# Pairs of feed-forward weight strips multiplied with seven block products in place of eight

## The chip, the core and the metric

The kernel runs on one core of one Trainium2 chip. The engines run on their own and wait for each other by semaphores: TensorE (PE; PEld is its weight load), VectorE (DVE), ScalarE (ACT), GpSimd (POOL), and SyncE (SP), which issues most transfers. Times are device microseconds from one execution of the program; of several, the median counts.

## The reference

One inference step of a trunk of two layers on 640 tokens (128 context, 512 latent), width 1024. A layer is a modulated norm, three token mixers side by side, a gated sum with an output projection, and then the part that the change touches:

```python
    h2 = modulated_norm(x, norm_ffn, shift2, scale2)
    f_gate, f_up = jnp.split(h2 @ w_ffn_in, 2, axis=-1)
    x = x + gate2[:, None, :] * ((jax.nn.silu(f_gate) * f_up) @ w_ffn_out)
```

`w_ffn_in` is 1024 x 5632 and `w_ffn_out` 2816 x 1024, all in float32. shift, scale and gate are six parts of `mod`, a product of the conditioning with `w_ada`.

## The kernel before

Tokens lie along the free axis (T = 640, two halves of 320) and features on the partitions, in KD = 8 blocks of 128. Weights come as 292 strips of 128x1024, each eight 128x128 blocks, through three buffers `wraw`, issued by SyncE in order (`strip_load`, L437); a strip waits until the one three before it is in use. For accuracy each float32 operand is split in a high part (rounded to fp32r) and a low part (the rest), and a product is three matmuls: high x high, high x low, low x high. GpSimd makes both parts of a strip: the copy L481 and the subtraction L483, whose result lies on `wraw` itself. For eight strips of layer 0's mixers ScalarE makes the high part (`HI_ON_ACT`).

The feed-forward stage of a layer works on 22 products c, in two parts f of 11. Product c takes a gate strip and an up strip, each 8 blocks x 3 matmuls x 2 halves = 48 matmuls into a pair of PSUM banks (`tiles_of`, L499). ScalarE takes the SiLU (L1401), VectorE multiplies by the up part (`gact`, L1915), ScalarE makes its high part `ahi` (L1403) and VectorE the low part `alo` (L1918). After 11 products come 11 strips of `w_ffn_out`, and VectorE adds each block m of the result to x (`add_to_x`, L1872). The first two strips of the stage run block by block behind the norm (`first_strips`, L509); the last block of the stage is done one half after the other (`last_tile`, also L509), so that the next norm can begin: its squares are summed on VectorE (L1432), and TensorE spreads the root (`norm_spread`, L578). In the norm VectorE scales (`tn`, L1451), ScalarE writes `hhi` (L1019) and VectorE `hlo` (L1461).

The modulation is computed by VectorE reductions over 128x1024 rows of `w_ada` (`ada_dot`, L1483), two for each of 48 blocks per layer. They stand in layer 0's mixers and, 48 blocks of them, in the feed-forward stages (`LATE`: the last 8 of layer 0 and 40 of layer 1 in layer 0's stage, the last 8 of layer 1 in layer 1's). Their loads are issued from ScalarE's queue.

All orders are written out by hand in each engine's program.

## Time and profile before

| | us |
|---|---|
| median of 3 timed runs (lowest, highest) | 2983.67 (2977.31, 2991.55) |
| profiled execution | 2975.47 |
| its span, first to last instruction | 2973.6 |
| PE busy in the span | 2823.4 (95%) |
| POOL, DVE, ACT busy | 1596.7, 1430.7, 754.1 |
| mean granted TensorE clock | 0.974 |

The page lists busy time by engine, then the chain of work that ended last, then groups of instructions by line. A duration on it is one profiled execution's. An engine's busy time counts waiting that happens inside an instruction, as for a port; the chain counts what the end waited for. In names such as `L483 POOL TENSOR_TENSOR wlo<-wraw,whi` the result stands ahead of the arrow. A strip product's stage is best read from a stretch that holds only it: 1146 to 1589 us is the feed-forward of layer 0, 967 to 1100 the merge and the output projection ahead of it.

### The profile page before, as it was taken

How to read it: one execution, taken by the hardware profiler on the slowest of the kernel's cores; microseconds unless marked ns; L12 is line 12 of the kernel's file. 1: busy time of each engine (PE TensorE's matmuls, PEld its weight loads, DVE VectorE, ACT ScalarE, POOL GpSimd, SP SyncE). 2: the span in 40 equal slices, each digit the busy share in tenths (PEclk: the TensorE clock that was granted, in tenths of full speed). 3: DMA queues.
4: the chain of work that ended last, by engine and by line, in shares of the span. 5: the costliest groups of instructions: out<-in, count | busy, mean ns of one | idle time of the engine just before them, and what ended most of it. 6: DMA issues, size and time to landing. Idle time of an engine off the chain costs nothing.

```text
span 2973.6 us, 42669 instructions
## 1 busy us (share of the span) xinstructions
PE 2823.4 (95%) x17704; PEld 2550.6 (86%) x17704; DVE 1430.7 (48%) x2267; ACT 754.1 (25%) x1411; POOL 1596.7 (54%) x596
## 2 busy tenths in 40 slices
PE   7889899989999999999999989999999999999998
PEld 2349687978888999999998869797988998999998
DVE  6555685664545235477646571542455425411113
ACT  3442112215564112000112110414555212000110
POOL 0426132364434776788875507075333675777775
PEclk9979999999999999999999999899999999999999
DMA  5422242231111323345422213021111233322222
GB/s 218 138 96 95 92 161 88 96 92 43 52 46 61 114 70 123 113 156 163 144 91 88 92 59 102 5 93 54 46 52 52 84 96 107 98 73 78 72 78 79
DMA packets 80093, 272.12 MB, mean 92 GB/s; under 512 B 8955, under 2 KB 14715, under 8 KB 78108
## 3 DMA queue, kind: packets, MB, share of 16 engines
q1 hardware_dynamic: 48124, 168.77, 17.8%
q10 hardware_dynamic: 31776, 100.62, 9.8%
q8 instruction: 140, 2.29, 0.3%
q14 instruction: 53, 0.43, 0.1%
HBM read 245.76 MB, written 23.59 MB: 91 GB/s over the span
## 4 chain that ended last, share of the span: by engine, by line
PE 80%; DVE 9%; ACT 4%; issue 2%; DVEq 1%; DMA 1%; POOLq 1%; POOL 1%; ACTq 0%; SPq 0%
PE PS L499 46%; PE PS L843 9%; PE PS L562 4%; PE PS L636 3%; PE PS L892 2%; PE PS L509 2%; PE PS L790 2%; DVE adap L1483 2%; PE PS L864 1%; PE PS L774 1%; POOLq L482 1%; PE PS L602 1%; POOL wlo L483 1%; PE PS L759 1%; PE PS L869 1%
## 5 line engine op out<-in xcount | busy, mean ns | idle before, releaser
L481 POOL TENSOR_SCALAR whi<-wraw 128x1024 fp32r<-128x1024 f32 x284 | 819.2, 2884 | 1146.6 <-PE PS L499 635.5
L483 POOL TENSOR_TENSOR wlo<-wraw,whi 128x1024 fp32r<-128x1024 f32 x292 | 734.4, 2515 | 83.3 <-ACT whi L1246 38.9
L499 PE MATMUL PS<-hhi,whi 128*128 128x320 f32 x2432 | 556.7, 310 | 15.7 <-POOL wlo L483 15.7
L499 PE MATMUL PS<-hhi,wlo 128*128 128x320 f32 x2432 | 554.7, 309 | 0.0
L499 PE MATMUL PS<-hlo,whi 128*128 128x320 f32 x2432 | 554.7, 309 | 0.0
L499 PEld LDWEIGHTS PS<-hhi,whi 128*128 128x128 f32 x2432 | 407.2, 188 | 18.4 <-POOL wlo L483 11.5
L499 PEld LDWEIGHTS PS<-hlo,whi 128*128 128x128 f32 x2432 | 407.8, 188 | 0.0
L499 PEld LDWEIGHTS PS<-hhi,wlo 128*128 128x128 f32 x2432 | 407.4, 188 | 0.0
L1483 DVE CUSTOM_DVE_ANT_0 adap<-ada,cond 128x1024 f32<-128x1024 f32 x176 | 333.2, 1893 | 36.1 <-DMA ada<-in_w_ada 14.7
L1401 ACT ACTIVATE silu<-PS 128x640 f32<-128x640 f32 x44 | 31.2, 708 | 659.1 <-PE PS L499 655.8
L1915 DVE TENSOR_TENSOR gact<-silu,PS 128x640 f32<-128x640 f32 x44 | 36.1, 821 | 333.3 <-ACT silu L1401 333.3
L1872 DVE SCALAR_TENSOR_TENSOR x<-PS,mod,x 128x128 f32<-128x128 f32 x144 | 54.9, 435 | 249.2 <-PE PS L499 241.2
L1315 ACT ACTIVATE dp<-PS,mx 128x640 f32<-128x640 f32 (+1 forms) x160 | 113.5, 710 | 238.5 <-DVE mx L1772 238.4
L1772 DVE TENSOR_REDUCE mx<-PS 128x2 f32<-128x1280 f32 (+1 forms) x80 | 102.2, 1278 | 145.8 <-PE PS L870 93.4
L843 PE MATMUL PS<-hhi,whi 128*128 128x320 f32 x512 | 172.2, 336 | 0.0
L843 PE MATMUL PS<-hhi,wlo 128*128 128x320 f32 x512 | 158.6, 310 | 0.0
L843 PE MATMUL PS<-hlo,whi 128*128 128x320 f32 x512 | 158.5, 310 | 0.0
L499 PE MATMUL PS<-ahi,whi 128*128 128x320 f32 x660 | 150.7, 309 | 0.9 <-POOL wlo L483 0.9
L499 PE MATMUL PS<-alo,whi 128*128 128x320 f32 x660 | 150.4, 309 | 0.0
L499 PE MATMUL PS<-ahi,wlo 128*128 128x320 f32 x660 | 150.3, 309 | 0.0
L499 PEld LDWEIGHTS PS<-ahi,whi 128*128 128x128 f32 x660 | 110.2, 188 | 1.5 <-issue 1.3
L499 PEld LDWEIGHTS PS<-alo,whi 128*128 128x128 f32 x660 | 110.4, 188 | 0.0
(294 smaller groups left out, 5022.8 us busy)
## 6 DMA issues: line engine op xcount, KB each, us to landing
wraw<-in_w_strips SPq DMA_DIRECT2D x292, 512.0 KB, 3.5
ada<-in_w_ada ACTq DMA_DIRECT2D x80, 512.0 KB, 4.6
spectra<-hst ACTq DMA_DIRECT2D x48, 256.0 KB, 2.1
hld<-spectra ACTq DMA_DIRECT2D x8, 768.0 KB, 5.0
hld<-spectra ACTq DMA_DIRECT2D x12, 512.0 KB, 3.6
part<-hacc ACTq DMA_DIRECT2D x8, 640.0 KB, 3.5
macc<-part ACTq DMA_DIRECT2D x8, 640.0 KB, 4.1
pada<-in_w_ada ACTq DMA_DIRECT2D x8, 512.0 KB, 3.7
```

The costliest lines, as they stand in the source:

```text
L481: nc.gpsimd.tensor_scalar(hi, raw, 1.0, None, ALU.mult)
L483: nc.gpsimd.tensor_tensor(lo, raw, hi, ALU.subtract).then_inc(w_split, 1)
L499: ins = pe.matmul(out[:, h, :], w[:, kt, :], mv[:, h * HALF:(h + 1) * HALF], start=start and m == 0, stop=stop and m == 2)
L509: ins = pe.matmul(pair(p)[:, h, :], w[:, kt, :], mv[:, h * HALF:(h + 1) * HALF], start=start and m == 0, stop=stop and m == 2)
L562: ins = pe.matmul(PS[:, i, :], hp[:, k, i * 128:(i + 1) * 128], w, start=(k == 0 and m == 0), stop=(k == KD - 1 and m == 2))
L636: ins = pe.matmul(out, w, h, start=(r == 0), stop=(r == len(terms) - 1))
L790: ins = pe.matmul(PS[:, 6 + qb % 2, hc], napt[n % 2][:, i, :], v, start=(i == 0), stop=(i == len(vs) - 1))
L843: ins = pe.matmul(out, w[:, kt, :], mv[:, k, cols], start=(k == i == 0), stop=(k == (3 if lift else 7) and i == 2))
L892: ins = pe.matmul(PS[:, 4, 128:192], dpt[:, i, :], v, start=(r == 0), stop=(r == len(vs) - 1))
L1315: ins = A(p[:, lo:640], PSF[:, DA_MAP * m + lo:DA_MAP * m + 640], ACT.Exp, bias=mx[:, q:q + 1], scale=-1.0, accum_out=sum2[:, 2 * n + m:2 ...
L1483: ins = V.tensor_tensor_reduce(adap[s][:, :], ada[s][j][:, :], cond[s][:, c, :], 1.0, 0.0, ALU.mult, ALU.add, mraw[:, 2 * m + c:2 * m + c ...
L1772: V.tensor_reduce(mx[:, q:q + 2], both[:, :, 0:keys], AX, ALU.min).then_inc(s_dm, 1)
```

## The change

Products c = 0 and 1 of a layer stay as they were. For the other 20, the gate and the up strip (two block rows, each two halves of 4 blocks) are multiplied with `h` (two halves of features, two of tokens) by the Winograd form of Strassen's scheme: seven block products "1" to "7" of 4 blocks x 3 matmuls x 320 columns, each into a PSUM bank of its own (`block_product`, eight banks in turn), in the order of `run_of`. For it:

- VectorE forms, once per layer, four sums of quarters of `h` (`h_sums`), from a full-precision copy `hf` that ScalarE writes in the norm beside `hhi`, and their low parts; for each pair of strips, one pair ahead, four sums of strip halves (`strip_sums`).
- ScalarE makes the high part of each block (`block_high`, four products ahead), GpSimd only the low part (four buffers each, `bhi`, `blo`). ScalarE also keeps product "1" in SBUF and takes SiLU on one half at a time.
- VectorE combines the seven banks (`pair_sums`): seven additions with a PSUM operand, two multiplications.

The stage has four parts of 6, 6, 5 and 5 products in place of two of 11, each followed by as many strips of `w_ffn_out`, so there are 32 additions to x per layer in place of 16. The last tile has 5 terms per half in place of 11. The modulation blocks of layer 1 move to the places in its mixers where layer 0 has its own, blocks 40 to 47 of each layer into its merge, and only 16 of layer 1 stay in layer 0's feed-forward stage. `HI_ON_ACT` covers both layers. Several start-up semaphores are merged (the one of the tables also counts `ones` and `wcol`; features with parameters; `cond` with `decay`).

```diff
 KF = DFF // 128
-KFH = KF // 2
+PARTS = (6, 6, 5, 5)
+PAIR0 = (0, 6, 12, 17, 22)
+PLAIN = 2
...
+LATE = [(1, m) for m in range(2 * KD)]
+
+HI_ON_ACT = [lay * STRIPS + n for lay in range(DEPTH) for n in range(S_NA + 4, S_NA + N_NA)]
...
+def run_of(f):
+
+    for c in range(max(PAIR0[f], PLAIN), PAIR0[f + 1]):
+        yield c, "1"
+        if c > max(PAIR0[f], PLAIN):
+            yield c - 1, "4"
+        for name in "25637":
+            yield c, name
+    yield PAIR0[f + 1] - 1, "4"
...
+            BANK[_lay, _c, _name] = (_r + BANK0[_f]) % 8
+            REUSED[_lay, _c, _name] = _run[_r - 8] if _r >= 8 else None
...
+        tsum = [at(f"tsum{i}", 40 + 10 * i, [128, KB, HALF]) for i in range(3)]
+        tlo = [at(f"tlo{i}", 40 + 10 * i, [128, KB, HALF], F32R) for i in range(3)]
+        thi = [at(f"thi{i}", 45 + 10 * i, [128, KB, HALF], F32R) for i in range(3)]
+        bsum = [at(f"bsum{i}", 108.75 + 2 * i, [128, KB, 128]) for i in range(3)]
+        bhi = [at(f"bhi{i}", 114.75 + 2 * i, [128, KB, 128], F32R) for i in range(4)]
+        blo = [at(f"blo{i}", k, [128, KB, 128], F32R) for i, k in enumerate((122.75, 148.75, 150.75, 152.75))]
...
+        def block_of(lay, c, name):
+
+            f = max(i for i in range(len(PARTS)) if PAIR0[i] <= c)
+            n = lay * STRIPS + S_IN[f] + 2 * (c - PAIR0[f])
+            first, second = wraw[n % 3], wraw[(n + 1) % 3]
+            g = 4 * (c - PLAIN)
+            came = [(w_in[m % 3], 16 * (m // 3 + 1)) for m in (n, n + 1)]
+            return {"1": (first[:, 0:4, :], came[0]), "2": (first[:, 4:8, :], came[0]),
+                    "5": (bsum[0][:, :, :], (w_add, nth(lay, w_add, g + 1))),
+                    "6": (bsum[1][:, :, :], (w_add, nth(lay, w_add, g + 2))),
+                    "3": (bsum[2][:, :, :], (w_add, nth(lay, w_add, g + 3))),
+                    "7": (second[:, 0:4, :], (w_add, nth(lay, w_add, g + 4))),
+                    "4": (second[:, 4:8, :], came[1])}[name]
...
             def strip_load(n):
 
-                if n >= 3:
-                    sp.wait_ge(w_used, n - 1)
+                if n - 3 in STARTED:
+                    sp.wait_ge(w_used, STARTED[n - 3] + 2)
+                elif n >= 3:
+                    sp.wait_ge(w_add, LAST_ADD[n - 3])
+                    sp.wait_ge(w_blo, LAST_LOW[n - 3] + 1)
...
+            for lay in range(DEPTH):
+                for idx in range(S_FFN + 2 * PLAIN):
+                    strip_split(lay * STRIPS + idx)
+                for f in range(len(PARTS)):
+                    for c, name in run_of(f):
+                        i = PRODUCTS[lay, c, name]
+                        pool.wait_ge(w_bhi, i + 1)
+                        nc.gpsimd.tensor_tensor(blo[i % 4][:, :, :], block_of(lay, c, name)[0], bhi[i % 4][:, :, :],
+                                                ALU.subtract).then_inc(w_blo, 1)
+                    for idx in range(S_IN[f] + 2 * PARTS[f], S_IN[f + 1]):
+                        strip_split(lay * STRIPS + idx)
...
+                def block_product(f, c, name):
+
+                    i = PRODUCTS[lay, c, name]
...
+                    bank = BANK[lay, c, name]
+                    pe.wait_ge(w_blo, i + 1)
+                    if REUSED[lay, c, name] is not None:
+                        pe.wait_ge(*bank_free(lay, *REUSED[lay, c, name]))
...
+                    if c == PLAIN and name in "5674":
+                        pe.wait_ge(s_tlo, nth(lay, s_tlo, "5674".index(name) + 1))
+                    for k in range(KB):
+                        hi, lo = (hhi[:, kt + k, cols], hlo[:, kt + k, cols]) if part is None else \
+                            (thi[part][:, k, :], tlo[part][:, k, :])
+                        for m, (w, mv) in enumerate(((bhi[i % 4], hi), (bhi[i % 4], lo), (blo[i % 4], hi))):
+                            ins = pe.matmul(PS[:, bank, 0:HALF], w[:, k, :], mv,
+                                            start=k == m == 0, stop=k == KB - 1 and m == 2)
+                            if name == "1" and c == max(PAIR0[f], PLAIN) and k == m == 0:
+                                ins.then_inc(w_used, 1)
+                    ins.then_inc(s_prod, 1)
+
+                for f, nk in enumerate(PARTS):
+                    for c, name in run_of(f):
+                        block_product(f, c, name)
...
                 ins.then_inc(s_hi, 1)
+                if nrm % 2:
+                    for sgm, cols in SEGMENTS[i // KD]:
+                        ins = A(hf[:, k, cols], tn[k % 3][:, cols], ACT.Identity, bias=mod[:, shift + k, sgm:sgm + 1])
+                    ins.then_inc(s_hf, 1)
...
+                def block_high(c, name):
+
+                    i = PRODUCTS[lay, c, name]
+                    src, came = block_of(lay, c, name)
+                    act.wait_ge(*came)
+                    if i >= 4:
+                        act.wait_ge(s_prod, i - 3)
+                    A(bhi[i % 4][:, :, :], src, ACT.Copy).then_inc(w_bhi, 1)
...
+                        act.wait_ge(s_tadd, nth(lay, s_tadd, 4))
+                        act.wait_ge(s_fi, nth(lay, s_fi, PLAIN))
+                        A(hhi[:, 0:KB, HALF:T], hf[:, 0:KB, HALF:T], ACT.Copy).then_inc(s_thi, 1)
+                    for i, (c, name) in enumerate(run):
+                        if name == "1":
+                            block_keep(c)
+                        if i + 4 < len(run):
+                            block_high(*run[i + 4])
+                        if name == "2":
+                            block_silu(c, 0)
+                        elif name == "3":
+                            block_silu(c, 1)
+                        elif name == "4":
+                            product_high(f, c)
...
+                    if i == 0:
+                        dve.wait_ge(s_cond[3], 16 * (lay + 1))
+                    for k in range(2 * i, 2 * i + 2):
+                        ada_dot(4, KD * lay + k, N_ADA2 + k)
+                modulation(lay, N_ADA2, N_ADA)
...
+                def strip_sums(c, which):
...
+                    dst, x0, x1, op, name = (
+                        (bsum[0][:, :, :], second[:, 0:4, :], second[:, 4:8, :], ALU.add, "5"),
+                        (bsum[1][:, :, :], bsum[0][:, :, :], first[:, 0:4, :], ALU.subtract, "6"),
+                        (bsum[2][:, :, :], first[:, 4:8, :], bsum[1][:, :, :], ALU.subtract, "3"),
+                        (second[:, 0:4, :], first[:, 0:4, :], second[:, 0:4, :], ALU.subtract, "7"))[which]
+                    if which < 2:
+                        m = n + 1 - which
+                        dve.wait_ge(w_in[m % 3], 16 * (m // 3 + 1))
+                    if g and which < 3:
+                        before = (lay, c - 1) if c > PLAIN else (lay - 1, KF - 1)
+                        dve.wait_ge(w_blo, PRODUCTS[before[0], before[1], name] + 1)
+                    dve.drain()
+                    V.tensor_tensor(dst, x0, x1, op).then_inc(w_add, 1)
...
+                def h_sums():
+
+                    b11, b12 = hf[:, 0:KB, 0:HALF], hf[:, 0:KB, HALF:T]
+                    b21, b22 = hf[:, KB:KD, 0:HALF], hf[:, KB:KD, HALF:T]
+                    dve.wait_ge(s_hf, nth(lay, s_hf, 16))
+                    V.tensor_tensor(tsum[0][:, :, :], b12, b11, ALU.subtract).then_inc(s_tadd, 1)
+                    V.tensor_tensor(tsum[2][:, :, :], b22, b12, ALU.subtract).then_inc(s_tadd, 1)
+                    dve.drain()
+                    V.tensor_tensor(tsum[1][:, :, :], b22, tsum[0][:, :, :], ALU.subtract).then_inc(s_tadd, 1)
+                    dve.drain()
+                    V.tensor_tensor(b12, b21, tsum[1][:, :, :], ALU.subtract).then_inc(s_tadd, 1)
...
+                def pair_sums(f, c):
+
...
+                    dve.wait_ge(s_snap, nth(lay, s_snap, c - PLAIN + 1))
+                    dve.wait_ge(*product_done(lay, c, "2"))
+                    V.tensor_tensor(g1[:, h0], first1[:, :], p2, ALU.add).then_inc(s_part, 1)
+                    if c > max(PAIR0[f], PLAIN):
+                        product_low(f, c - 1)
+                    if more:
+                        strip_sums(c + 1, 0)
+                        strip_sums(c + 1, 1)
+                    dve.drain()
+                    dve.wait_ge(*product_done(lay, c, "6"))
+                    V.tensor_tensor(mid[:, :], first1[:, :], p6, ALU.add).then_inc(s_part, 1)
+                    dve.drain()
+                    V.tensor_tensor(g1[:, h1], mid[:, :], p5, ALU.add).then_inc(s_part, 1)
+                    if more:
+                        strip_sums(c + 1, 2)
+                    dve.drain()
+                    dve.wait_ge(*product_done(lay, c, "3"))
+                    V.tensor_tensor(g1[:, h1], g1[:, h1], p3, ALU.add).then_inc(s_part, 1)
+                    dve.wait_ge(*product_done(lay, c, "7"))
+                    V.tensor_tensor(mid[:, :], mid[:, :], p7, ALU.add).then_inc(s_part, 1)
+                    dve.drain()
+                    V.tensor_tensor(gate2[:, :], mid[:, :], p5, ALU.add).then_inc(s_part, 1)
+                    if more:
+                        strip_sums(c + 1, 3)
+                    dve.drain()
+                    dve.wait_ge(s_psilu, nth(lay, s_psilu, 2 * (c - PLAIN) + 2))
+                    V.tensor_tensor(g1[:, h1], g1[:, h1], gate2[:, :], ALU.mult)
+                    dve.wait_ge(*product_done(lay, c, "4"))
+                    V.tensor_tensor(mid[:, :], mid[:, :], p4, ALU.add).then_inc(s_part, 1)
+                    dve.drain()
+                    V.tensor_tensor(g1[:, h0], g1[:, h0], mid[:, :], ALU.mult).then_inc(s_gact, 1)
+
+                h_sums()
+                plain_product(0)
+                for i in range(3):
+                    h_sum_low(i)
+                product_low(0, 0)
+                for i in range(4):
+                    strip_sums(PLAIN, i)
+                plain_product(1)
+                product_low(0, 1)
+                h_sum_low(3)
+                for f, nk in enumerate(PARTS):
+                    for c in range(max(PAIR0[f], PLAIN), PAIR0[f + 1]):
+                        pair_sums(f, c)
+                    product_low(f, PAIR0[f + 1] - 1)
+                    last = f == len(PARTS) - 1
...
+                        if m == KD - 1:
+                            for i in range(4):
+                                strip_sums(PAIR0[f + 1], i)
...
+                        add_to_x(m, OUT_PAIRS[f][m], 40, s_xf)
+                        if lay == 0 and m < LATE_DOTS[f]:
```

GpSimd, in the products of part 0. Before, two instructions for a strip, four for a product, with `whi` and `wlo` of 1024 columns:

```order
L481 TENSOR_SCALAR whi_53<-wraw_50 128x1024
L483 TENSOR_TENSOR wlo_55<-wraw_50,whi_53 128x1024
L481 TENSOR_SCALAR whi_54<-wraw_51 128x1024
L483 TENSOR_TENSOR wlo_56<-wraw_51,whi_54 128x1024
L481 TENSOR_SCALAR whi_53<-wraw_52 128x1024
L483 TENSOR_TENSOR wlo_57<-wraw_52,whi_53 128x1024
```

After, seven in a row of part 0: block products "1" of c = 3, "4" of c = 2, then "2", "5", "6", "3" and "7" of c = 3. Each has 512 columns; `bsum` are sums of strip halves, `wraw` the strips' own halves (or, for "7", the fourth sum, which lies there):

```order
L579 TENSOR_TENSOR blo_241<-wraw_52,bhi_237 128x512
L579 TENSOR_TENSOR blo_242<-wraw_51,bhi_238 128x512
L579 TENSOR_TENSOR blo_239<-wraw_52,bhi_235 128x512
L579 TENSOR_TENSOR blo_240<-bsum_232,bhi_236 128x512
L579 TENSOR_TENSOR blo_241<-bsum_233,bhi_237 128x512
L579 TENSOR_TENSOR blo_242<-bsum_234,bhi_238 128x512
L579 TENSOR_TENSOR blo_239<-wraw_50,bhi_235 128x512
```

Copies of the raw strip have gone from this engine, and one subtraction stands for each block product.

VectorE, in the products of part 0 before (layer 0; `ISA` are the modulation's reductions, `adap` their scratch result):

```order
L1483 ISA mraw 128x1
L1483 ISA adap_128,mraw<-ada_118,cond_124 128x1024
L1483 ISA mraw 128x1
L1483 ISA adap_128,mraw<-ada_118,cond_124 128x1024
L1483 ISA mraw 128x1
L1915 TENSOR_TENSOR gact_205<-silu_203,PS 128x640
L1918 TENSOR_TENSOR alo<-gact_205,ahi 128x640
L1483 ISA adap_128,mraw<-ada_119,cond_124 128x1024
L1483 ISA mraw 128x1
L1483 ISA adap_128,mraw<-ada_119,cond_124 128x1024
L1483 ISA mraw 128x1
```

After, for c = 2 of layer 0, from behind the addition of product "2" to the last multiplication; `first`, `mid` and `gate` are halves of 320 columns:

```order
L2085 TENSOR_TENSOR bsum_232<-wraw_50 128x512
L2085 TENSOR_TENSOR bsum_233<-bsum_232,wraw_52 128x512
L2146 TENSOR_TENSOR mid<-first_221,PS 128x320
L2148 TENSOR_TENSOR gact_217<-mid,PS 128x320
L2085 TENSOR_TENSOR bsum_234<-wraw_52,bsum_233 128x512
L2153 TENSOR_TENSOR gact_217<-gact_217,PS 128x320
L2155 TENSOR_TENSOR mid<-mid,PS 128x320
L2157 TENSOR_TENSOR gate_219<-mid,PS 128x320
L2085 TENSOR_TENSOR wraw_50<-wraw_52,wraw_50 128x512
L2162 TENSOR_TENSOR gact_217<-gact_217,gate_219 128x320
L2164 TENSOR_TENSOR mid<-mid,PS 128x320
L2166 TENSOR_TENSOR gact_217<-gact_217,mid 128x320
```

The two operations per product have become fourteen: these twelve, `gact<-first,PS` ahead of them, and the low part of the previous product. Four of them are sums for the next pair, and the reductions are gone from here.

## Rows read from the trace of the kernel before

**Rows 1.** The page's first part: busy time, share of the span, instructions

```profile
PE 2823.4 (95%) x17704; PEld 2550.6 (86%) x17704; DVE 1430.7 (48%) x2267; ACT 754.1 (25%) x1411; POOL 1596.7 (54%) x596
```

**Rows 2.** Sums by stretch: us, then each engine's busy us (instructions), PEclk, DMA share, GB/s

```profile
967.00:1100.00 133.00, 133.00 (x909) 133.00 (x908) 36.15 (x49) 17.86 (x25) 99.50 (x38) 1.00 0.30 96
...
1146.00:1589.00 443.00, 442.13 (x3012) 441.28 (x3011) 249.29 (x288) 37.53 (x52) 347.85 (x125) 1.00 0.40 127
```

**Rows 3.** The chain that ended last: start us, us, what

```profile
248.05 63.63 PE PS L499 x432
...
700.91 1.81 PE PS L843 x12
...
966.73 133.76 PE PS L499 x912
...
1621.20 72.21 PE PS L499 x480
...
2336.03 133.77 PE PS L499 x912
```

**Rows 4.** The page's costliest groups

```profile
L483 POOL TENSOR_TENSOR wlo<-wraw,whi 128x1024 fp32r<-128x1024 f32 x292 | 734.4, 2515 | 83.3 <-ACT whi L1246 38.9
...
L1915 DVE TENSOR_TENSOR gact<-silu,PS 128x640 f32<-128x640 f32 x44 | 36.1, 821 | 333.3 <-ACT silu L1401 333.3
L1872 DVE SCALAR_TENSOR_TENSOR x<-PS,mod,x 128x128 f32<-128x128 f32 x144 | 54.9, 435 | 249.2 <-PE PS L499 241.2
```

**Rows 5.** Groups by line and shape: busy us, mean ns of one, idle before

```profile
L1641 DVE TENSOR_TENSOR yt<-PS,hld 128x512 f32<-128x512 f32 x80 | 49.7, 684 | 18.3 <-PE PS L707 11.8 <-DMA hld<-spectra 5.0 <-issue 0.4
...
L1918 DVE TENSOR_TENSOR alo<-gact,ahi 128x640 fp32r<-128x640 f32 x44 | 36.3, 825 | 35.4 <-ACT ahi L1403 35.4
...
L1811 DVE TENSOR_TENSOR hsig<-hsig,PS 128x320 f32<-128x320 f32 x32 | 15.4, 481 | 5.4 <-PE PS L843 4.8 <-issue 0.5
...
L1131 ACT ACTIVATE hst<-PS 128x512 f32<-128x512 f32 x24 | 14.3, 594 | 18.0 <-PE PS L636 15.2 <-ACT hst L1131 1.8 <-ACT pada L1079 0.9
```

**Rows 6.** Timelines of GpSimd and VectorE: merge 1026 to 1029, product 1251 to 1259

```profile
1026.28 2.39 POOL L483 TENSOR_TENSOR wlo<-wraw,whi 128x1024 fp32r<-128x1024 f32 x1
...
1026.60 0.82 DVE L1860 TENSOR_TENSOR sig<-sig,PS 128x640 f32<-128x640 f32 x1 [13.91 <-PE PS L499]
1027.50 1.85 DVE L1862 TENSOR_TENSOR macc<-macc,sig 128x640 f32<-128x640 f32 x1
...
1251.43 2.77 POOL L481 TENSOR_SCALAR whi<-wraw 128x1024 fp32r<-128x1024 f32 x1 [1.14 <-PE PS L499]
1254.35 2.41 POOL L483 TENSOR_TENSOR wlo<-wraw,whi 128x1024 fp32r<-128x1024 f32 x1
1258.47 3.35 POOL L481 TENSOR_SCALAR whi<-wraw 128x1024 fp32r<-128x1024 f32 x1 [1.71 <-PE PS L499]
...
1253.52 0.82 DVE L1918 TENSOR_TENSOR alo<-gact,ahi 128x640 fp32r<-128x640 f32 x1 [0.80 <-ACT ahi L1403]
1254.48 3.35 DVE L1483 CUSTOM_DVE_ANT_0 adap<-ada,cond 128x1024 f32<-128x1024 f32 x1
...
1257.96 1.22 DVE L1483 CUSTOM_DVE_ANT_0 adap<-ada,cond 128x1024 f32<-128x1024 f32 x1
```

**Rows 7.** Timeline of ScalarE in the norm ahead of the feed-forward

```profile
1119.55 0.75 ACT L1019 ACTIVATE hhi<-tn,mod 128x128 fp32r<-128x128 f32 x2 [0.43 <-DVE tn L1451]
```

**Rows 8.** Timeline of TensorE at the start of the stage

```profile
1137.55 0.56 PE L499 MATMUL PS<-hhi,whi 128*128 128x320 f32 x2 [2.10 <-POOL wlo L483]
```

**Rows 9.** The chain at the end of layer 0

```profile
1580.87 7.71 PE PS L509 x51
...
1589.14 2.31 PE PS L509 x15
```

**Rows 10.** Timeline of VectorE at the end of layer 0

```profile
1587.26 0.49 DVE L1432 TENSOR_TENSOR ssum<-ssum,sq 128x320 f32<-128x320 f32 x1 [0.61 <-ACT sq L1007]
...
1589.73 0.56 DVE L1440 TENSOR_TENSOR rdiag<-ident,rcol 128x384 f32<-128x384 f32 x1
```

457 lines of the change are left out of this document (250 added, 207 removed).

## The prediction

> **What bounds the kernel now.** I read the page's first part, then sums by stretch, then the chain that ended last, then the groups of instructions, and last the timeline of one product. The first says TensorE, 95% of the span [rows 1]. The sums by stretch say how hard: in layer 0's feed-forward stretch TensorE issues 3012 matmuls in 443 us, busy for 442 at a clock of 1.00, and layer 1's is like it [rows 2]. In the chain the ordinary strip product (L499) takes 133.76 us for 912 matmuls, 0.1467 each [rows 3]. There are 22 products (c) per layer in the first projection; one is 96 matmuls, so 14.08 us, without an idle moment. VectorE does two operations of 0.82 us for it [rows 4, 5], ScalarE two short ones. GpSimd is the busy neighbour: 348 of 443 us [rows 2]. The reader should see that fewer matmuls shorten this stage, and that GpSimd and VectorE have room only while they don't get in each other's way.
>
> **What goes.** 20 of the 22 products of a layer become seven block products of 4 x 3 matmuls over 320 columns: 84 in place of 96. Two layers: 40 x 12 = 480 matmuls fewer, 480 x 0.1467 = 70.4 us. All that follows is taken off that. Twelve matmuls into one half bank take 1.81 us in the chain, pipeline's end included [rows 3], so staying in one bank costs nothing against alternating between two. A pair of strips would take 84 x 0.1467 = 12.32 us, one block product 1.76.
>
> **What a pair asks of the others.** ScalarE: seven copies of 128x512 (0.59 for such a size [rows 5]) and four activations of half to the whole of 640 columns, some 6.6 us of 12.3, so covered. GpSimd: seven subtractions of 128x512. No row has that size; twice the size takes 2.35 to 2.41 [rows 6]. The bounds for half are 1.2 (nothing fixed) and 2.35 (all fixed); with the 0.14 us that VectorE's rows leave fixed (0.48 for 320 columns, 0.82 for 640 [rows 5]) it would be 1.27. I take 1.2, near the lower end, plus the 0.15 us that lie between two of its instructions (1254.20 to 1254.35 [rows 6]): 7 x 1.35 = 9.5 us. VectorE: four strip sums of 0.68, seven additions of a PSUM bank and two multiplications of 0.48, one low part of 0.82 [rows 5]: 7.9 us, with 14 gaps of 0.1 us 9.3.
>
> **What they cost each other.** Here the change is risky. At 1254.48 a VectorE reduction with two SBUF inputs starts 0.13 us behind a GpSimd subtraction and takes 3.35 us in place of 1.22: it ends 1.07 us behind the subtraction's end. The GpSimd copy that starts during the next reduction takes 3.35 in place of 2.77 [rows 6]. So the two exclude each other when both read SBUF that way. Operations with a PSUM operand don't: L1860 takes its 0.82 us inside the subtraction of 1026.28 [rows 6]. The Trainium skill (SBUF — State Buffer, "Who interferes with whom") has this as an exclusive lock, held for the whole GpSimd instruction. This trace agrees for the subtraction and not for the copy: L1918 (two SBUF inputs) starts 2.09 us into a 2.77 us copy and still takes 0.82 [rows 6]. By the page the port is held for 10.4 us per product before and 8.4 after, and the change would relieve it; by the rows mainly the two subtractions (4.8 us) hold it before, and the change nearly doubles that. The sum below is the same by both, since no copy is left on GpSimd in a pair.
>
> After the change all seven GpSimd instructions of a pair are of the kind that blocks, and seven of VectorE's operations have two SBUF inputs (four sums, two multiplications, the low part). How long one of these holds the port I take from how far it ends behind the GpSimd instruction that it waited for: macc (640 columns) starts at 1027.50, in the subtraction that ends at 1028.67, and ends 0.68 behind it [rows 6]; 0.35 for 320 and 0.55 for 512 in proportion. That is 4 x 0.55 + 2 x 0.35 + 0.68 = 3.6 us. GpSimd's round is then 9.5 + 3.6 = 13.1 us if VectorE uses none of its gaps, and 12.0 if it uses all. VectorE's round: 9.3 us, and seven waits. One that comes at random waits for half an instruction two times in three (0.4), the two sums that follow another operation of the kind at once wait for nearly a whole one (1.0): 5 x 0.4 + 2 x 1.0 = 4.0, together 13.3. Against it stand eight banks and four block buffers, with which VectorE may fall some 2 to 4 us behind before TensorE starves, and it catches up at the end of each part, where there is no next pair to sum for. Between 12.32 and 13.2 I take 12.6 us per pair: 40 x (14.08 - 12.6) = 59 us gained.
>
> **What is added around it**, in both layers unless said:
> - Start of the stage. In the norm ScalarE now writes each block twice. In the first half it works for 0.75 us of each step and idles for 0.43 [rows 7]; twice 0.64 (two back to back) and a semaphore, about 1.4, is more than the 1.18 that VectorE sets now: 8 x 0.2, and about as much in the second half: 3 us. Behind it TensorE already waits for GpSimd, 2.10 us at 1137.55 [rows 8]. Now four sums over 1280 columns (1.49 us each, by the step from 320 to 640 columns [rows 5]) and the low parts fall beside these splits and hold them up by one or two sums: 2 to 3 us. Together 5.3, twice: 10.6. Bounds 4 and 24: little of it shows, or the first sums of strips also come late for product 5.
> - Four handovers to the second projection per layer, not two. GpSimd can split the first output strip only behind the last block's low part, about 5.0 us before TensorE is done with the blocks (four block products ahead, less ScalarE's copy and the subtraction), and needs 2.77 + 0.15 + 2.41 = 5.3 [rows 6], more with VectorE in between. 1 us each, 8 together; bounds 2 and 28 (3.5 us each where GpSimd has no lead).
> - The last tile has 5 terms per half and not 11: 18 matmuls (2.64 us) less cover behind half 0. Before, half 0 was done 33 matmuls after 1580.87, at 1585.7, and the root was spread behind the 15 matmuls that end at 1591.45 [rows 9], 5.7 us later. The squares are summed at 1587.75, and the diagonal is ready at 1590.29, 1.7 us behind TensorE's sums that followed 1588.58 [rows 9, 10]: 2.0 + 1.7 and two semaphores, the spread can stand 4.2 us behind half 0, 1.5 earlier. Net 1.2 per layer, 2.4.
> - The modulation products move. Of layer 1 they now stand in its own mixers, as in layer 0. Layer 0 takes 718.7 us from its first strips to the merge (248.05 to 966.73), layer 1 714.8 (1621.20 to 2336.03) [rows 3]: 4 us is the price. Eight per layer (16 reductions) move into the merge, where VectorE is busy for 36 of 133 us and GpSimd for 99.5 [rows 2]; at most 16 x 1.07 = 17 us of blocking fit into the 33 that are left: 1 us. Their loads move on ScalarE's queue, each behind the use of its slot.
> - Merged start-up semaphores: up to 1 us, I take none. The 22 output strips keep their matmuls; 16 more additions to x, of three parts of 0.435 us [rows 4], lie beside 5 us of TensorE each.
>
> Sum: -59 + 10.6 + 8 + 2.4 + 4 + 1 = -33 us. The profiled execution took 2975.5 us (span 2973.6), so it would take 2942.5. The median of the timed runs is 2983.7, 8.2 above it; the same step from there gives 2951 us, my forecast.
>
> **Rivals.**
> - TensorE stays the bound throughout (12.32 per pair) and the costs lie near their lower bounds (12 us): -70 + 12 = -58, 2926 us. For it speak the buffers; against it that GpSimd and VectorE are both within 1 us of the round.
> - The saving is eaten at the seams: 13.1 us per pair, starts and handovers at twice my prices: -39 + 36 = -3, 2981 us, no change. For it: the start of the stage has its waits already [rows 8].
> - The shared port becomes the bound, and the kernel slower. Place: the seven GpSimd subtractions of a pair. If an instruction has 0.3 us that don't shrink with its size, it takes 1.02 + 0.3 + 0.15 = 1.47, and the round is 10.3 + 3.6 = 13.9: 40 x 0.18 = 7 us gained, 26 paid, +19, 3003 us. It decides from 13.4 us per pair on (40 x 0.65 = 26): from 1.25 us per subtraction if VectorE uses none of the gaps, 1.4 if all. Against it: no row shows such a fixed part, but no row excludes it, since all subtractions have one size.
> - It doesn't do what it says: the matmuls are fewer, but each block's low part comes late and TensorE idles for as long. In time that is the port's case, and its chance counts there.
>
> **Chances.** Forecast (2934 to 2968 as its own range) 0.52, TensorE bound 0.10, seams 0.22, port 0.16. A measurement of this kernel can tell 0.5% (15 us) from no change. Faster by more than that: 0.48 + 0.10 + 0.08 = 0.66; within: 0.04 + 0.13 + 0.02 = 0.19; slower: 0.01 + 0.14 = 0.15. The range of 2926 to 2998 leaves out most of the port's case and a little below.
>
> **What will show it.** PE's count of matmuls falls by 480. Right: 12.6 us or so from one pair to the next; the GpSimd subtraction of 512 columns at 1.2 us undisturbed; VectorE's strip sums up to 1.8; TensorE's idle time in the stage below 25 us per layer, ended by GpSimd. Wrong: a subtraction above 1.3 us; a round of 13.4 or more; TensorE idle for want of a bank (VectorE as releaser); a start of the stage more than 10 us longer. If layer 1's mixers take clearly more than layer 0's, the comparison of layers was no guide.

## The result

| | median us (lowest, highest; runs) | ratio to the kernel before, 95% interval |
|---|---|---|
| before, same sessions | 2982.39 (2974.92, 2991.55) | |
| changed kernel | 2993.76 (2985.98, 3000.23; 20) | 1.0037 [1.0027, 1.0046] |

No gain: 11 us, or 0.4%, slower, where 2951 us was forecast. The spans of the two profiled executions are 11.5 us apart (2985.1 and 2973.6), so the trace shows what the clock shows.

### The profile page after: what moved, and what is told of

It reads as the page before. It is cut to its first block, busy times and chain, and to the rows that moved or that the text cites. A ratio compares the mean times of both kernels' runs of the same rounds, so it can differ in the third digit from the quotient of the medians.

```text
span 2985.1 us, 43757 instructions
## 1 busy us (share of the span) xinstructions
PE 2775.7 (93%) x17224; PEld 2492.3 (83%) x17224; DVE 1890.8 (63%) x2861; ACT 962.6 (32%) x1835; POOL 1590.7 (53%) x708
## 3 DMA queue, kind: packets, MB, share of 16 engines
q1 hardware_dynamic: 48124, 168.77, 18.2%
## 4 chain that ended last, share of the span: by engine, by line
PE 62%; DVE 17%; POOL 7%; ACT 5%; issue 3%; DVEq 3%; DMA 2%; POOLq 1%; ACTq 0%; SPq 0%
PE PS L598 26%; PE PS L938 9%; POOL blo L579 4%; PE PS L1078 4%; PE PS L659 3%; DVE adap L1652 3%; PE PS L733 3%; PE PS L987 2%; PE PS L885 2%; DVE bsum L2085 2%; POOL wlo L570 1%; DMA ada<-in_w_ada 1%; PE PS L608 1%; PE PS L959 1%; DVE gact L2162 1%
## 5 line engine op out<-in xcount | busy, mean ns | idle before, releaser
L568 POOL TENSOR_SCALAR whi<-wraw 128x1024 fp32r<-128x1024 f32 x196 | 567.7, 2896 | 1005.7 <-PE PS L598 493.2
L598 PE MATMUL PS<-hhi,whi 128*128 128x320 f32 x1152 | 266.9, 313 | 21.4 <-POOL wlo L570 21.4
L598 PE MATMUL PS<-hlo,whi 128*128 128x320 f32 x1152 | 265.1, 311 | 0.0
L598 PE MATMUL PS<-hhi,wlo 128*128 128x320 f32 x1152 | 264.7, 311 | 0.0
L579 POOL TENSOR_TENSOR blo<-wraw,bhi 128x512 fp32r<-128x512 f32 x160 | 244.1, 1548 | 25.0 <-ACT bhi L1526 25.0
L598 PEld LDWEIGHTS PS<-hhi,whi 128*128 128x128 f32 x1152 | 194.9, 190 | 23.7 <-POOL wlo L570 12.7
L1078 PE MATMUL PS<-hhi,bhi 128*128 128x320 f32 x640 | 198.0, 309 | 0.3 <-POOL blo L579 0.2
L1078 PE MATMUL PS<-hhi,blo 128*128 128x320 f32 x640 | 197.8, 309 | 0.0
L598 PEld LDWEIGHTS PS<-hlo,whi 128*128 128x128 f32 x1152 | 195.2, 190 | 0.0
L598 PEld LDWEIGHTS PS<-hhi,wlo 128*128 128x128 f32 x1152 | 195.1, 190 | 0.0
L598 PE MATMUL PS<-ahi,whi 128*128 128x320 f32 x684 | 158.9, 314 | 18.2 <-POOL wlo L570 18.2
L938 PE MATMUL PS<-hhi,whi 128*128 128x320 f32 x512 | 172.3, 337 | 0.0
L938 PE MATMUL PS<-hlo,whi 128*128 128x320 f32 x512 | 158.7, 310 | 0.0
```

The source lines that it names most:

```text
L568: nc.gpsimd.tensor_scalar(hi, raw, 1.0, None, ALU.mult)
L579: nc.gpsimd.tensor_tensor(blo[i % 4][:, :, :], block_of(lay, c, name)[0], bhi[i % 4][:, :, :], ALU.subtract).then_inc(w_blo, 1)
L598: ins = pe.matmul(out[:, h, :], w[:, kt, :], mv[:, h * HALF:(h + 1) * HALF], start=start and m == 0, stop=stop and m == 2)
L938: ins = pe.matmul(out, w[:, kt, :], mv[:, k, cols], start=(k == i == 0), stop=(k == (3 if lift else 7) and i == 2))
L1078: ins = pe.matmul(PS[:, bank, 0:HALF], w[:, k, :], mv, start=k == m == 0, stop=k == KB - 1 and m == 2)
```

## The profile after

From the page: engines, then the shares of the chain that ended last, then the two groups of GpSimd's block subtractions.

```profile
PE 2775.7 (93%) x17224; PEld 2492.3 (83%) x17224; DVE 1890.8 (63%) x2861; ACT 962.6 (32%) x1835; POOL 1590.7 (53%) x708
...
PE 62%; DVE 17%; POOL 7%; ACT 5%; issue 3%; DVEq 3%; DMA 2%; POOLq 1%; ACTq 0%; SPq 0%
...
L579 POOL TENSOR_TENSOR blo<-wraw,bhi 128x512 fp32r<-128x512 f32 x160 | 244.1, 1548 | 25.0 <-ACT bhi L1526 25.0
L579 POOL TENSOR_TENSOR blo<-bsum,bhi 128x512 fp32r<-128x512 f32 x120 | 189.9, 1605 | 107.2 <-ACT bhi L1526 107.2
```

The 480 matmuls are gone (17224 for 17704 in [rows 1]), and PE is 48 us less busy. In the chain PE falls from 80% on the page before to 62%, and VectorE takes 17% in place of 9%. Sums by stretch (busy us of PE, PEld, DVE, ACT, POOL, then clock), the feed-forward of layer 0 and layer 1's mixers:

```profile
1140.00:1590.00 450.00, 425.43 (x2844) 420.13 (x2844) 353.04 (x465) 130.81 (x242) 353.13 (x189) 0.99 0.29 91
1618.00:2347.00 729.00, 688.81 (x4346) 607.97 (x4347) 430.22 (x727) 250.78 (x491) 295.03 (x109) 0.97 0.25 81
```

In [rows 2] TensorE worked 442 of 443 us; now 425 of 450. One round of a pair, VectorE first (start, duration, operation), then GpSimd:

```profile
1271.57 1.62 DVE L2085 TENSOR_TENSOR bsum<-wraw 128x512 f32<-128x512 f32 x1
1273.28 1.61 DVE L2085 TENSOR_TENSOR bsum<-bsum,wraw 128x512 f32<-128x512 f32 x1
1274.99 0.49 DVE L2146 TENSOR_TENSOR mid<-first,PS 128x320 f32<-128x320 f32 x1
1275.57 0.49 DVE L2148 TENSOR_TENSOR gact<-mid,PS 128x320 f32<-128x320 f32 x1
1276.15 1.70 DVE L2085 TENSOR_TENSOR bsum<-wraw,bsum 128x512 f32<-128x512 f32 x1
1277.94 0.49 DVE L2153 TENSOR_TENSOR gact<-gact,PS 128x320 f32<-128x320 f32 x1
1278.34 0.48 DVE L2155 TENSOR_TENSOR mid<-mid,PS 128x320 f32<-128x320 f32 x1
1278.91 0.49 DVE L2157 TENSOR_TENSOR gate<-mid,PS 128x320 f32<-128x320 f32 x1
1279.49 0.69 DVE L2085 TENSOR_TENSOR wraw<-wraw,wraw 128x512 f32<-128x512 f32 x1
1280.27 1.40 DVE L2162 TENSOR_TENSOR gact<-gact,gate 128x320 f32<-128x320 f32 x1
1281.59 0.47 DVE L2164 TENSOR_TENSOR mid<-mid,PS 128x320 f32<-128x320 f32 x1
1282.16 1.02 DVE L2166 TENSOR_TENSOR gact<-gact,mid 128x320 f32<-128x320 f32 x1
1283.10 0.47 DVE L2138 TENSOR_TENSOR gact<-first,PS 128x320 f32<-128x320 f32 x1
1283.98 1.04 DVE L2119 TENSOR_TENSOR alo<-gact,ahi 128x640 fp32r<-128x640 f32 x1 [0.41 <-ACT ahi L1547]
1285.11 1.61 DVE L2085 TENSOR_TENSOR bsum<-wraw 128x512 f32<-128x512 f32 x1
```

```profile
1271.02 6.28 POOL L579 TENSOR_TENSOR blo<-wraw,bhi 128x512 fp32r<-128x512 f32 x4 [0.22 <-ACT bhi L1526]
1279.53 4.81 POOL L579 TENSOR_TENSOR blo<-bsum,bhi 128x512 fp32r<-128x512 f32 x3 [2.23 <-ACT bhi L1526]
1284.55 1.62 POOL L579 TENSOR_TENSOR blo<-wraw,bhi 128x512 fp32r<-128x512 f32 x1 [0.21 <-ACT bhi L1526]
```

The round is 13.54 us (1271.57 to 1285.11), and VectorE has no pause in it but the 0.41 us for ScalarE's `ahi`. Undisturbed, its operations take 0.69 (sum), 0.49 (addition, multiplication) and 0.82 (low part); the three long sums, the two multiplications and the low part together take 4.5 us more. So VectorE's list is 9.0 us of its own, with the gaps and that pause, and 4.5 of waiting. GpSimd's seven subtractions take 11.1 us of the round (6.28 + 4.81) for 9.0 undisturbed, and it idles 2.4 us. The other rows are the handovers and starts, and one gap in layer 1's mixers that was 0.8 us before:

```profile
1210.16 0.56 PE L598 MATMUL PS<-ahi,whi 128*128 128x320 f32 x2 [2.28 <-POOL wlo L570]
```

```profile
1140.04 0.50 PE L598 MATMUL PS<-hhi,whi 128*128 128x320 f32 x1 [3.22 <-POOL wlo L570]
...
2007.50 0.79 PE L659 MATMUL PS<-whi,hhi 128*128 128x512 f32 x1 [8.34 <-ACT draw L1414]
```

And from the chain, to set beside [rows 3] and the start of [rows 8]: the first 49 matmuls of the stage's ordinary strips, and the mixers of layer 1, which now last from 1618.26 to 2346.99.

```profile
1140.04 9.01 PE PS L598 x49
...
1618.26 72.12 PE PS L598 x480
...
2346.99 35.20 PE PS L598 x240
```

The last rows are two stretches of output strips, in the same sums as above (the last number but two is the clock). Both follow a wait of 2.27 or 2.28 us:

```profile
1210.00:1252.60 42.60, 42.44 (x289) 42.44 (x290) 32.28 (x50) 3.16 (x5) 33.22 (x14) 1.00 0.44 136
1333.00:1377.00 44.00, 43.66 (x287) 43.66 (x288) 32.07 (x50) 2.98 (x5) 32.72 (x14) 0.96 0.41 132
```

## The experiments

Theory A, after this first look: the shared port. GpSimd's seven subtractions and VectorE's operations with two SBUF inputs exclude each other, and what they cost each other makes the round. Its rival in the first four runs is that GpSimd's own speed sets it. A second theory, V, came up on the way: VectorE's list, in its fixed order, is what closes the round, and the port counts only by what it adds there.

Medians of the experiments come from four sessions, in which the kernel before took 2981.0 to 2984.3 us; the ratios compare within one. The other four columns are from the profiled executions, by TensorE's stretches, in us. "Pair" is the time from first to last block product over all eight parts, divided by 40, so it also holds a part's first pairs, which still go at TensorE's pace. A profiled execution isn't always a typical one: that of e1 took 2978.0 us, the lowest of its twelve and 14 below their median, those of e14 and e15 are 7 below theirs, and that of the changed kernel, too, is 7 below.

| kernel | median us | ratio, 95% interval | pair us | handovers, 8 together | output strips | layer 1's mixers |
|---|---|---|---|---|---|---|
| changed | 2993.8 | 1.0037 [1.0027, 1.0046] | 13.08 | 18.2 | 309.1 | 728.5 |
| e1 SiLU later | 2992.1 | 1.0022 [1.0008, 1.0036] | 12.84 | 21.5 | 305.7 | 725.2 |
| e2 half subtraction | 2937.1 | 0.9835 [0.9816, 0.9854] | 12.38 | 0 | 303.1 | 723.2 |
| e3 copy | 2940.0 | 0.9844 [0.9823, 0.9864] | 12.35 | 5.3 | 303.1 | 722.8 |
| e4 first output strip on ScalarE | 2980.6 | 0.9991 [0.9977, 1.0004] | 13.10 | 0 | 317.2 | 724.0 |
| e5 small reductions | 2974.9 | 0.9975 [0.9965, 0.9986] | 13.12 | 18.2 | 307.7 | 711.8 |
| e6 short sums | 2949.3 | 0.9896 [0.9880, 0.9913] | 12.38 | 3.2 | 303.1 | 732.1 |
| e7 e1, and low part of 1 on VectorE | 3002.4 | 1.0066 [1.0048, 1.0084] | 13.31 | 14.4 | 312.3 | 732.6 |
| e8 e7 and e4 | 2988.8 | 1.0022 [1.0010, 1.0033] | 13.15 | 0 | 312.9 | 728.6 |
| e9 e8, low part later | 2989.1 | 1.0022 [1.0010, 1.0034] | 13.31 | 0 | 313.4 | 728.1 |
| e10 24 blocks back | 3024.8 | 1.0145 [1.0129, 1.0161] | 13.18 | 18.2 | 327.0 | 707.7 |
| e11 e9 and e10 | 3022.5 | 1.0144 [1.0128, 1.0160] | 13.55 | 0 | 329.2 | 710.9 |
| e12 e1, e4 and e10 | 2994.8 | 1.0041 [1.0027, 1.0056] | 12.87 | 0 | 321.7 | 709.4 |
| e13 one addition less | 2977.9 | 0.9978 [0.9967, 0.9989] | 12.71 | 18.2 | 312.3 | 732.2 |
| e14 eight blocks back | 2956.5 | 0.9905 [0.9890, 0.9920] | 12.88 | 0 | 304.5 | 715.6 |
| e15 e14, SiLU as it was | 2984.0 | 1.0002 [0.9992, 1.0013] | 13.10 | 0 | 318.8 | 714.4 |

**e1** (ScalarE's second SiLU behind the block for "7", not "3"):

```diff
-                        elif name == "3":
+                        elif name == "7":
                             block_silu(c, 1)
```

> ScalarE's SiLU of the second half stands one step later, behind the high part of the next pair's product 5, so that GpSimd no longer idles 2.2 us per pair for that copy. Everything else as in the changed kernel (round of 13.54 us per pair). Theory A (GpSimd and the wait for ScalarE bound the round): the idle time closes, the round falls to 12.6 to 12.8, 40 x 0.8 = 32 us less, ratio to the changed kernel about 0.989. Theory B (VectorE's own work plus its waits for the port bound it: it is busy without a pause over the round): what GpSimd gains in idle time comes back as waits of VectorE, round 13.2 to 13.5, 0 to 14 us less.

In the trace the pairs became 0.24 us shorter, 9.6 us in all: VectorE's low part takes 0.82 us there in place of 1.04, and its round 13.36. The handovers became 3.3 longer. The ratio moved by 0.0015, with intervals that overlap: alone, the edit's worth is not settled (e15 settles it in company).

**e2 and e3** (the low part over 256 of 512 columns from a layer's second pair on; or, in place of the subtraction, a one-input operation that copies the block, so that the low parts are wrong data of the right size):

```diff
-                        nc.gpsimd.tensor_tensor(blo[i % 4][:, :, :], block_of(lay, c, name)[0], bhi[i % 4][:, :, :],
-                                                ALU.subtract).then_inc(w_blo, 1)
+                        nc.gpsimd.tensor_scalar(blo[i % 4][:, :, :].rearrange("p k n -> p (k n)"),
+                                                block_of(lay, c, name)[0].rearrange("p k n -> p (k n)"), 1.0, None,
+                                                ALU.mult).then_inc(w_blo, 1)
```

> GpSimd's subtraction covers 256 of the 512 columns (all but the first four of each layer), so half of each low part keeps older values; all else as in the changed kernel. Theory B (port waits of VectorE): a GpSimd instruction of 0.65 in place of 1.28 us halves the waits of 4.5 us per round, VectorE's round falls to 11.3 and TensorE bounds at 12.32 to 12.4: 40 x 1.15 = 46 us less, and TensorE's waits for a low part go. Theory C (VectorE's chain of semaphores with TensorE and ScalarE bounds, whatever the port): round stays above 13, less than 20 us gained. It also tells what part of 1.28 us does not shrink: 0 gives 0.64, the fixed 0.14 of VectorE's rows 0.71.

> GpSimd's subtraction is replaced by a one-input copy of the same 512 columns (the low parts are then copies of the raw block). Theory L (the port is held for the whole of any GpSimd instruction): a copy of 1.4 us (half of 2.77) holds VectorE up as the subtraction did, round 13.5 or more, no gain. Theory R (a copy holds it only in its first third, as L1918 in the trace before started 2.09 us into a 2.77 us copy): VectorE's strip sums fall from 1.6 to 1.0 us or less, the round to 12.3 to 12.8, 30 to 48 us less.

Both bring the pair to TensorE's 12.35 us and take 54 to 57 us off. GpSimd's groups in 50 us of e2, then in e3, and VectorE's in e3:

```profile
L580 POOL TENSOR_TENSOR blo<-bsum,bhi 128x256 fp32r<-128x256 f32 x12 | 9.6, 796 | 12.2 <-ACT bhi L1527 12.2
```

```profile
L579 POOL TENSOR_SCALAR blo<-bsum 128x512 fp32r<-128x512 f32 x12 | 18.5, 1546 | 3.2 <-ACT bhi L1527 3.2
```

```profile
L2120 DVE TENSOR_TENSOR alo<-gact,ahi 128x640 fp32r<-128x640 f32 x4 | 3.3, 819 | 0.0
...
L2086 DVE TENSOR_TENSOR bsum<-wraw 128x512 f32<-128x512 f32 x3 | 2.8, 923 | 0.3
```

In e3 GpSimd's operation is longer (1.49 us undisturbed, for 1.28), GpSimd is busier than in the changed kernel (366 of the 450 us, for 353), and TensorE never waits in a pair: GpSimd's own speed wasn't the bound. VectorE's sums take 0.69 to 0.92 us in that stretch (1.15 at the most in the whole run) in place of 1.62. The lock that costs a whole subtraction isn't there for this operation.

**e4** (ScalarE makes the high part of each part's first output strip, between two blocks, so that GpSimd has only its subtraction of 2.4 us to make behind the last block):

> ScalarE makes the high part of the first output strip of each part (four per layer), so that GpSimd has only the low part to make at the handover. Theory: the 2.27 us that TensorE waits at each of the eight handovers for GpSimd's 2.74 us copy go, 15 to 20 us less than the changed kernel, round unchanged at 13.54. Rival (the low part of the last products holds the handover up, which waits for VectorE): the wait falls by less than 1 us each, under 8 us.

The eight waits of 2.28 us are gone, but the output strips take 8 us longer. What is late next is VectorE's low part of the last product of the part:

```profile
1219.93 0.41 PE L599 MATMUL PS<-ahi,whi 128*128 128x320 f32 x1 [0.98 <-DVE alo L2122]
```

13 us net by the medians, 10 by the two traces, not 18.

**e5** (layer 1's 48 reductions in its own mixers over 8 columns):

```diff
+                    wd = 8 if (s == 1 and n >= 16) or (s == 3 and n >= KD) else D
-                    ins = V.tensor_tensor_reduce(adap[s][:, :], ada[s][j][:, :], cond[s][:, c, :], 1.0, 0.0,
+                    ins = V.tensor_tensor_reduce(adap[s][:, 0:wd], ada[s][j][:, 0:wd], cond[s][:, c, 0:wd], 1.0, 0.0,
```

> The changed kernel, in which the 48 modulation reductions that stand in layer 1's own mixers (blocks 16 to 39) go over 8 of 1024 columns; their loads stay. Layer 1's modulation is therefore not what the reference has. Its mixers (first strips to merge) took 728.7 us in the changed kernel's profile and 714.6 before. Theory M (the reductions on VectorE stand in the mixers' way, and that is what moving them cost): 715 to 719 us, total 10 to 14 us below the changed kernel, about 2982. Rival S (the 14 us are another thing: the loads on ScalarE's queue, the high parts that ScalarE now makes for layer 1 too, the lower clock): the mixers stay at 726 or more, total within 3 us of 2994.

711.8 us in place of 728.5: the reductions are the cause, at 17 us. Half of it is one place, the 8.34 us gap at 2007.50, which is 0.79 here.

**e6** (strip sums over one of four blocks, so most sums are incomplete):

> The changed kernel with VectorE's strip sums over one of their four blocks (128 of 512 columns) from the second pair on, so the products get wrong blocks in part; GpSimd's seven subtractions per pair stay whole. If the shared port bounds the round together with VectorE's order (theory P), VectorE's four waits become short, and its round falls by 4 x 0.5 of own work: pairs at 12.35 us, handovers 0 to 1.5 us each: 2994 - 29 - 8 to 18 = 2945 to 2957. If GpSimd's subtractions bound it by their own pace (theory G: 7 x 1.43 = 10.0 us plus the waits for ScalarE), nothing changes in the round: 2985 to 2994.

12.38, with all of GpSimd's subtractions in place. So shortening VectorE's operations at the port does as well as shortening GpSimd's. Neither e2, e3 nor e6 can tell port and list apart: each shortens both.

**e7, e8, e9** (VectorE makes the low part of product "1", one of GpSimd's seven, except in a part's first pair; e1's edit is in all three, e4's in e8 and e9. In e7 and e8 the new operation stands behind the first two strip sums; e9 puts it later, as the cut shows):

```diff
                     if more:
+                        i = PRODUCTS[lay, c + 1, "1"]
+                        dve.wait_ge(w_bhi, i + 1)
+                        V.tensor_tensor(blo[i % 4][:, :, :], block_of(lay, c + 1, "1")[0], bhi[i % 4][:, :, :],
+                                        ALU.subtract).then_inc(s_tlo, 1)
                         strip_sums(c + 1, 2)
```

> The changed kernel with two edits: ScalarE takes the second SiLU two products later, and the low part of product 1 (16 of 20 pairs per... of each layer's pairs that aren't a part's first) is made by VectorE and no more by GpSimd. Theory P (the port is the scarce thing: GpSimd's seven subtractions of 1.28 us and VectorE's 3.6 us that need it): six subtractions and 0.55 us more on VectorE are 7.7 + 4.2 = 11.9 us, below the 12.35 of TensorE, so pairs at 12.4 to 12.6 us in place of 13.08: 2994 - 20 to 27 = 2967 to 2974. Rival V (VectorE's list in its fixed order is the bound, and one more operation of 0.7 to 1.6 us makes it longer): 13.2 to 13.8 us per pair, 2998 to 3015.

> Both edits of the run before, and ScalarE makes the high part of each part's first output strip, so that GpSimd needn't. By theory P the handovers fall from 2.3 us to near nothing, 11 to 14 us more (the same edit alone gave 13): 2953 to 2963, 1 to 1.5% faster than the changed kernel and about 1% faster than the kernel before. By rival V 2985 to 3000.

> The three edits of the last run, but VectorE's low part of product 1 stands after the sum for product 5 (1.7 products later in the list, TensorE needs it four block products after that) in place of before product 6's addition, where TensorE waited for it 0.97 and 1.44 us in two pairs of the run before last. Theory P (the port): with TensorE no longer waiting for this part, GpSimd's six subtractions and VectorE's operations fit below 12.35: 12.4 to 12.7 us per pair in all parts, 2952 to 2966 us in all. Rival V (VectorE's list with its waits is the bound, wherever the operation stands): 13.0 us per pair or more in most parts, 2980 to 2995.

I had bet on the port, and this is where that fell. Less on the port by the sum of uses, and the kernel is slower: e7 is 10 us above e1, e8 8 us above e4. VectorE in e9:

```profile
1285.38 0.68 DVE L2167 TENSOR_TENSOR blo<-wraw,bhi 128x512 fp32r<-128x512 f32 x1
...
1294.88 1.61 DVE L2100 TENSOR_TENSOR bsum<-wraw 128x512 f32<-128x512 f32 x1
1296.58 1.61 DVE L2100 TENSOR_TENSOR bsum<-bsum,wraw 128x512 f32<-128x512 f32 x1
...
1299.27 0.68 DVE L2167 TENSOR_TENSOR blo<-wraw,bhi 128x512 fp32r<-128x512 f32 x1
```

```profile
1286.12 0.42 PE L1091 MATMUL PS<-hhi,bhi 128*128 128x320 f32 x1 [0.96 <-DVE blo L2167]
```

Its round is 13.89 us, for 13.36 in e1: the list has one entry more. And TensorE, which by my count would need this part four block products later, stands waiting when it comes, because VectorE runs that far behind.

But the same list has more than one length. In e8 two parts of layer 1 went at 12.35 us per pair, one of them with 504 matmuls in 74.08, while the same part of layer 0 took 80.74; in e7 the last part of layer 0 did. VectorE in the fast part of e8:

```profile
2685.31 1.61 DVE L2100 TENSOR_TENSOR bsum<-wraw 128x512 f32<-128x512 f32 x1
2687.02 0.69 DVE L2100 TENSOR_TENSOR bsum<-bsum,wraw 128x512 f32<-128x512 f32 x1
2687.63 0.69 DVE L2161 TENSOR_TENSOR blo<-wraw,bhi 128x512 fp32r<-128x512 f32 x1
...
2694.49 0.49 DVE L2183 TENSOR_TENSOR mid<-mid,PS 128x320 f32<-128x320 f32 x1 [0.32 <-PE PS L1091]
...
2696.32 0.49 DVE L2153 TENSOR_TENSOR gact<-first,PS 128x320 f32<-128x320 f32 x1 [0.64 <-PE PS L1091]
...
2697.63 1.62 DVE L2100 TENSOR_TENSOR bsum<-wraw 128x512 f32<-128x512 f32 x1
```

Here the round is 12.32 us, VectorE waits about 1 us for TensorE in it, and only two of its sums are long (1.61 and 1.45). In the slow part (round from 1294.51 to 1308.53, 14.02 us) the second sum takes 1.62 and the low part 1.76. So the time lost at the port isn't fixed by how many operations need it, but by how the two engines' operations meet, round after round. What puts a part into one pattern or the other isn't settled.

**e10 to e12** (layer 1's blocks 16 to 39 back in layer 0's feed-forward stage, two behind each output block; e11 has e9's edits too, e12 e1's and e4's):

> The changed kernel, but layer 1's blocks 16 to 39 of the modulation are back in layer 0's feed-forward stage: 40 blocks there (12, 12, 12, 4 per part, two behind each output block's addition) and none of these in layer 1's mixers. Theory M: layer 1's mixers fall from 728 to 711 to 715 us, the output strips of layer 0 become 0 to 8 us longer (48 more reductions of 1.07 us beside GpSimd's subtractions): 2978 to 2988. Rival (they cost as much where they go, since VectorE's reductions hold up GpSimd's splits, on which the output strips wait): 2990 to 3000.

> The edits of the two runs before together. If both theories hold the gains add: 2994 - 30 to 40 - 6 to 16, so 2940 to 2958 us, 1 to 1.4% faster than the kernel before. If only the reductions' part holds, 2970 to 2985; if neither, 2985 to 3000.

> The changed kernel with three edits: second SiLU two products later, ScalarE makes the high part of each part's first output strip, the reductions back in layer 0's feed-forward stage. All seven low parts of a pair stay on GpSimd. Sum of the single gains measured so far (-2 to -9, -13, and -6 to -16 by theory M): 2956 to 2973 us. If VectorE's move of one low part is what counts, this is 10 to 20 us above the run before; if it is worth nothing, the two agree within 5 us.

The mixers fell by 21 us, a little more than expected; what I had left out is the queue in the new place. Two blocks are four reductions, 4.9 us undisturbed (x 1.22), with the addition's 1.1 more than TensorE's 5.3 us per output block (42.5 / 8), so VectorE falls behind; ScalarE waits in order for each `ada` slot before it may split the next part's blocks, and TensorE waits for those. ScalarE, then TensorE in e10:

```profile
1227.87 43.45 ACTq L1163 DMA_DIRECT2D ada<-in_w_ada  x12
1271.43 1.15 ACT L1527 ACTIVATE bhi<-wraw 128x512 fp32r<-128x512 f32 x2 [52.59 <-DVE mraw L1653]
```

```profile
1273.97 0.64 PE L1078 MATMUL PS<-hhi,bhi 128*128 128x320 f32 x1 [13.68 <-POOL blo L579]
```

Three such gaps (13.68, 6.30 and 9.83) make 30 us. The kernel before has 48 blocks in this stage (56 in the two stages together) without such a gap, but there most of them (64 of 96 reductions in layer 0's stage) run beside the products, not beside the output strips.

**e13** (one of seven PSUM additions less; no port in it):

```diff
-                    V.tensor_tensor(gate2[:, :], mid[:, :], p5, ALU.add).then_inc(s_part, 1)
-                    V.tensor_tensor(g1[:, h1], g1[:, h1], gate2[:, :], ALU.mult)
+                    V.tensor_tensor(g1[:, h1], g1[:, h1], mid[:, :], ALU.mult)
```

> The changed kernel without one of VectorE's seven additions per pair with a PSUM operand (mid + p5): the second multiplication takes mid itself, so the up half misses product 5. The addition needs no port (0.49 us and 0.09 ahead of it). Theory V (VectorE's list with its waits closes the round): 13.54 - 0.58 = 12.96 us per round in steady state, 8 pairs... of 10 full rounds a layer or more 0.58 less, so 40 x 0.4 to 0.58 = 16 to 23 us below the changed kernel: 2971 to 2978. Theory P (the sum of the port's uses, 7 x 1.28 + 3.6 and the gaps, closes it): the round stays at 13.4 or more, total 2988 to 2994.

This is the run that tells V from the port. TensorE's waits for product "5" are 13.02 us apart (1298.62, 1311.64), 0.52 less than in the changed kernel (1294.91, 1308.46: 13.55), for an operation of 0.58 with its gap. All else in the round is as it was: the three long sums still take 1.60 to 1.71 us, the two multiplications 1.41 and 1.02, and GpSimd idles the same 2.4 us. The median is 16 us lower.

**e14 and e15** (three edits: e1's, e4's, and only blocks 16 to 23 back, one behind each output block; e15 without e1's):

```diff
-LATE_DOTS = (6, 6, 4, 0)
+LATE_DOTS = (7, 7, 7, 3)
-LATE = [(1, m) for m in range(2 * KD)]
+LATE = [(1, m) for m in range(N_ADA1)]
...
+                        elif i + 4 == len(run):
+                            strip_hi(lay * STRIPS + S_IN[f] + 2 * PARTS[f])
```

> The changed kernel with three edits: second SiLU two products later; ScalarE makes the high part of each part's first output strip; layer 1's modulation blocks 16 to 23 (the eight that stand ahead of the differential attention's projections) go back to layer 0's feed-forward stage, one block behind each output block (7, 7, 7 and 3 per part). In the changed kernel TensorE idles 8.3 us at 1999.16 to 2007.5 in layer 1, and 0.8 there in the kernel before. Expected: that gap gone (-7 to -9), handovers -11 to -13, SiLU -2 to -9, the output strips of layer 0 at most 3 us longer: 2964 to 2976 us. If the eight blocks cost as much in the new place: 2975 to 2985.

> The run before without the move of the SiLU. If the SiLU's place is worth what its trace showed (pairs of 12.84 in place of 13.08 us, 40 x 0.24 = 9.6), this is 5 to 10 us slower than the run before; if it is worth what the medians showed (2 us), the two agree within 4 us.

e14 beats both kernels: 2956.5 us, 0.9905 [0.9890, 0.9920] of the kernel before. Its sums by stretch, to set beside those above (layer 0's feed-forward, layer 1's mixers):

```profile
1140.00:1575.00 435.00, 418.14 (x2813) 414.14 (x2814) 361.53 (x485) 134.54 (x241) 337.78 (x185) 1.00 0.34 105
1612.00:2329.00 717.00, 681.59 (x4345) 601.50 (x4346) 400.44 (x694) 250.48 (x491) 294.16 (x109) 0.99 0.23 77
```

The SiLU's place, worth 0 to 9 us alone, is worth 27 here. The traces give 23 of them: 0.22 x 40 = 9 in the pairs, 14 in the output strips (318.8 to 304.5), where e15 waits 0.97, 0.99, 1.83 and 1.86 us per layer for VectorE's last low part and e14's layer 0 has one such wait, of 1.23. A VectorE less far behind pays twice. Without e4's edit part of it, 3.3 of 9.6 us, is lost again in the handover (e1: 21.5 for 18.2).

## Why the prediction was wrong

**The step that failed: "Between 12.32 and 13.2 I take 12.6 us per pair."** Measured 13.08, 19 of the 43 us between forecast and median. The mechanism was right: VectorE's fixed list, its own work and its waits at the port, is longer than TensorE's round. Its parts were good, too: own work 9.3 us for 9.0, waits 4.0 for 4.5, together 13.3 for 13.5. What was mis-sized is what that costs. Buffers pay for a lag once. By the prediction's own numbers VectorE lags 0.98 us more with each pair (13.3 against 12.32), 39 us over 40 pairs, and eight parts absorb 2 to 4 us each, so 7 to 23 us are left: 12.5 to 12.9 us per pair, in the middle 12.7. Measured, the lag is 1.22 us per pair (13.54), 49 in all; TensorE lost 30, so 18 were absorbed, 2.3 per part. Of the 19 us the longer round makes 10, the smaller help of the buffers 6, the choice of 12.6 in place of 12.7 the rest. TensorE shows it: the wait of about 0.96 us per pair sets in with the third pair of a part (1185.27; 1281.38 with 0.56), and then stays. That the estimate of 4.0 us came so near is in part luck: it averaged over chance meetings, while e8 has rounds with 2 us of such waits and others with 4.4.

**GpSimd's price** was 1.28 us per subtraction, where I took 1.2 (1.27 with a fixed part: from e2's 0.74 for half of it, 0.2 is fixed). It didn't matter: GpSimd idles 2.4 us per round. The rival that made it the bound named the right mechanism in the wrong place; its limit, slower from 13.4 us per pair, held for the steady round, yet the average of 13.08 alone would still have left a gain of 40.

**Handovers**, 1 us each, 8 together: 2.28 each, 18.2. I reckoned with GpSimd about 5 us ahead of TensorE behind the last block. With the pairs at TensorE's pace it was: in e6 its copy of the first output strip starts at 1207.50, 5.0 us ahead of TensorE's last block product, and TensorE waits 0.40. With VectorE behind, in the changed kernel, it starts at 1204.85, 3.0 us ahead.

**Modulation, "4 us is the price"**: 13.9. The comparison of layers was the error that I had named as a risk, and the rows were misread: in [rows 3] layer 0 starts at 248.05 with x432 and layer 1 at 1621.20 with x480. The first 48 matmuls of layer 0 lie ahead of its row. Three rows of the kernel before:

```profile
240.29 0.41 PE L499 MATMUL PS<-hhi,whi 128*128 128x320 f32 x1 [2.10 <-POOL wlo L483]
...
626.75 0.80 PE L562 MATMUL PS<-whi,hhi 128*128 128x512 f32 x1 [7.58 <-ACT draw L1296]
...
1996.81 0.50 PE L562 MATMUL PS<-whi,hhi 128*128 128x512 f32 x1 [0.79 <-ACT draw L1296]
```

From 240.29 on layer 0 takes 726.4 us to the merge, and layer 1 714.8: 11.6 us, not 4. Up to the 384 matmuls that begin at 392.75 and 1775.14 the two are level (152.5 and 153.9); behind them layer 0 takes 574.0 us to the merge and layer 1 560.9. That difference, 13.1 us, was there to be read, half of it in one gap (7.58 against 0.79), and is what the edit cost. e5 gives 17 us, e10 21.

**Output strips**, which the prediction left at no price ("keep their matmuls"): 5.3 us. 2052 matmuls at 0.1467 are 301.0 us, and from start to start they take 6.8 more; the kernel before loses 1.5 there. Behind four of the eight handover waits the granted clock is below full: 0.96 over 1333 to 1377 us, where 288 matmuls take 43.9, and 1.00 over 1210 to 1252.6, where they take 42.3. The wait ahead is the same in both (2.27 and 2.28 us). In e2, e3 and e6, whose waits are 0.66 us or less, the clock stays at 1.00 in all eight.

**Starts**: 10.6 predicted, 5.5 measured. From the merge's end to the first ordinary strip it is 1.2 and 2.5 us more, and the first 96 matmuls there take 15.9 in place of 15.0 in each layer. Part of it is the clock: behind a wait of 3.22 us in place of 2.10 [rows 8], the first 49 matmuls take 9.01 us, 0.184 each, where [rows 3] have 0.147; over 1140 to 1144 us the granted clock is 0.57, and 1.00 in the kernel before.

**Tails and merge**: 2.4 and 1 predicted. Behind layer 0's last tile TensorE waits 2.82 + 4.70 us, 3.4 before. With the 36 matmuls (5.3 us) taken off that no longer lie there, the tails are 4.6 and 1.7 us longer, 6.3 in all. The merge is 1.2 us longer per layer, 2.4.

The sum: -40 + 18.2 + 13.9 + 5.3 + 5.5 + 6.3 + 2.4 = +11.6, for 11.5 measured. Of the 43 us that were missed, 19 lie in the round, 10 in the handovers, 10 in the modulation, 5 in the output strips and 5 in the tails and the merge; the starts gave 5 back. Handovers and modulation could be had back (e14), the round only in part.

Of the rivals, the one of the seams came nearest: 13.1 us per pair, handovers at twice their price. Its sum was wrong: starts and handovers twice (37.2) and the rest (7.4) are 44.6 us, not 36, so it should have said +5 and 2989 us.

## What to carry to other kernels

Where an engine serves another, compare its whole round, own work plus waits at a shared port, with the other's; if it is longer, buffers absorb the lag once per part, and from then on the time follows the round. A fixed list of operations is as much a bound as an engine at 100%: taking off one that needs no port gained its length (0.52 us of 0.58), and moving work onto that list lost more, in most parts, than it freed elsewhere. How long the waits in such a list are depends on how the engines meet, and can differ from part to part in one execution (e8). And a difference between two layers is the price of an edit only if both stretches start at the same matmul; the counts in the rows (x432 and x480) tell.

## What the hardware showed that was not expected

- GpSimd's one-input operation (here a multiplication by 1) does not lock VectorE out for its whole length: in e3 it takes 1.49 us for 128x512 and is itself drawn out to 1.65 to 1.87 beside VectorE's sums, which take 0.69 to 0.92. The two-input subtraction takes 1.28 us and makes the same sums 1.62. The slower instruction made the kernel 54 us faster. The Trainium skill (SBUF — State Buffer, "Who interferes with whom") has the shared pair as held for the whole instruction by whoever comes first; for the one-input form these rows do not show that.
- GpSimd's subtraction has a fixed part: 0.74 us for 256 columns and 1.28 for 512, so 0.2 us.
- An addition with one operand in PSUM takes 0.47 to 0.49 us in all 280 cases of the changed kernel, beside GpSimd or not.
- The same wait of 2.27 us left the granted clock at 1.00 behind four handovers and lowered it behind four others (0.72 over 1333 to 1337 us). What decides isn't shown.
